# Hybrid decoder block: the first norm applied behind the first eight products instead of ahead of them

## The reference

```python
h  = rms_norm(x, norm_mix_w)             # x: 512 rows of 1024
proj = h @ w_in                          # gdn q k v z alpha beta, fox q k v f o, merge gates
qkv = silu(causal_depthwise_conv(concat(gq, gk, gv), conv_w))   # 4 taps, 24 tiles of 128 channels
...                                      # gated delta rule, forgetting attention, merge,
x = x + y @ w_out                        # second norm, SwiGLU, final norm
...
def rms_norm(x, w):                      # y = x * rsqrt(mean(x*x) + EPS) * w, by row
```

## Time and profile before

| | us |
|---|---|
| median of 3 runs (lowest to highest) | 1158.74 (1158.58 to 1159.56) |
| the profiled execution | 1158.56 |
| its span, first to last instruction | 1157.0 |
| TensorE busy | 1133.6 (98%) |
| VectorE, ScalarE, GpSimd busy | 526.9, 454.6, 551.1 |
| mean granted clock of TensorE | 0.999 of 2.4 GHz |

### The profile page before, as it was taken

One profiled execution on the slowest core, in us unless ns is written; L12 is line 12 of the kernel. 1 busy time (PEld: TensorE's weight loads), 2 busy tenths in 40 slices (PEclk: granted clock), 3 DMA queues, 4 the chain that ended last, 5 costly groups with the idle time before them and its releaser, 6 DMA issues.

```text
span 1157.0 us, 16593 instructions
## 1 busy us (share of the span) xinstructions
PE 1133.6 (98%) x5973; PEld 943.3 (82%) x5973; DVE 526.9 (46%) x1135; ACT 454.6 (39%) x744; POOL 551.1 (48%) x297
## 2 busy tenths in 40 slices
PE   6999999999999999999999999999999999999997
PEld 5778888888888888888888888887888888888886
DVE  4434446464738257777777662523333333330001
ACT  5354353434344365555555432234223323321112
POOL 5434456362626155556566554434444444434443
PEclk9999999999999999999999999999999999999999
DMA  6333333231313243323323273523333333322231
GB/s 195 85 85 99 91 100 98 68 92 55 101 56 92 73 123 87 99 83 94 95 86 95 73 236 109 149 88 87 96 91 102 97 91 99 101 91 91 92 109 73
DMA packets 169632, 113.61 MB, mean 98 GB/s; under 512 B 6257, under 2 KB 157922, under 8 KB 169586
## 3 DMA queue, kind: packets, MB, share of 16 engines
q1 hardware_dynamic: 163218, 98.26, 29.8%
q10 hardware_dynamic: 6368, 14.72, 3.5%
HBM read 104.54 MB, written 8.42 MB: 98 GB/s over the span
## 4 chain that ended last, share of the span: by engine, by line
PE 86%; DVE 5%; issue 4%; POOL 3%; ACT 1%; DMA 1%; SPq 0%; DVEq 0%; ACTq 0%; POOLq 0%
PE ps L1465 61%; PE ps L1879 10%; PE ps L1555 6%; PE ps L1447 4%; PE ps L1771 2%; POOL w_lo L558 1%; PE ps L1738 1%; DVE ps L1180 1%; PE ps L1739 1%; DVE prod L1190 1%; POOL probs L651 1%; PE ps L1815 1%; DVE Wb L1195 1%; PE ps L1509 1%; DMA prm_rows<-in_gdn_norm_w 1%
## 5 line engine op out<-in xcount | busy, mean ns | idle before, releaser
L558 POOL TENSOR_TENSOR w_lo<-raw,w_hi 128x1024 fp32r<-128x1024 f32 x170 | 416.4, 2449 | 521.7 <-ACT w_hi L685 521.7
L1465 PE MATMUL ps<-h_hi,w_hi 128*128 128x512 f32 x976 | 384.6, 394 | 1.0 <-POOL w_lo L558 1.0
L1465 PE MATMUL ps<-h_hi,w_lo 128*128 128x512 f32 x976 | 384.0, 393 | 0.0
L1465 PE MATMUL ps<-h_lo,w_hi 128*128 128x512 f32 x976 | 383.0, 392 | 0.0
L685 ACT ACTIVATE w_hi<-raw 128x1024 fp32r<-128x1024 f32 x170 | 180.2, 1060 | 468.1 <-PE ps L1465 368.6
L1465 PEld LDWEIGHTS ps<-h_hi,w_hi 128*128 128x128 f32 x976 | 183.5, 188 | 39.6 <-issue 1.9
L1465 PEld LDWEIGHTS ps<-h_hi,w_lo 128*128 128x128 f32 x976 | 183.4, 188 | 36.8 <-issue 0.2
L1465 PEld LDWEIGHTS ps<-h_lo,w_hi 128*128 128x128 f32 x976 | 183.5, 188 | 36.1
L1056 DVE SCALAR_TENSOR_TENSOR tmp<-ps,prm,tmp 128x511 f32<-128x511 f32 (+2 forms) x72 | 53.9, 748 | 80.5 <-ACT tmp L715 75.4
L651 POOL TENSOR_SCALAR probs<-probs,rsum 128x128 f32<-128x128 f32 (+1 forms) x64 | 70.3, 1117 | 13.4 <-DVE rsum L1285 12.6
L1025 DVE TENSOR_SCALAR ms<-ss 128x1 f32<-128x1 f32 x8 | 1.2, 154 | 126.5 <-ACT raw L998 117.4
(11 more groups left out here) (268 smaller groups left out, 1557.1 us busy)
## 6 DMA issues: line engine op xcount, KB each, us to landing
raw<-in_w_in SPq DMA_DIRECT2D x80, 512.0 KB, 3.9
raw<-in_w_gate SPq DMA_DIRECT2D x22, 512.0 KB, 3.8
raw<-in_w_up SPq DMA_DIRECT2D x22, 512.0 KB, 3.8
raw<-in_w_down SPq DMA_DIRECT2D x22, 512.0 KB, 3.3
gate_dram<-gate ACTq DMA_DIRECT2D x24, 256.0 KB, 2.0
cumb<-cum_dram ACTq DMA_DIRECT2D x8, 512.0 KB, 3.5
raw<-in_w_branch_a SPq DMA_DIRECT2D x8, 512.0 KB, 3.9
raw<-in_w_branch_b SPq DMA_DIRECT2D x8, 512.0 KB, 3.9
```

Source lines behind the costliest of these rows:

```text
L558: pool.tensor_tensor(w_lo[:, r % 2, :], raw[:, r, :], w_hi[:, r % 2, :], ALU.subtract)\
L1465: return pe.matmul(ps[:, bank, :], wts[wl][k], acts[xl][:, k, :], start=(n == 0), stop=(n == len(PASSES) - 1))
```

## The change

The turned x is no longer normed ahead of its use. The blocks of x are turned as they are, split into new halves `hr_hi` and `hr_lo` (norm weight included, row factor not), and the first eight units (convs 0 and 1 with r from 0 to 3) and the small unit work on those. Their results are scaled by the row factors on the way out: VectorE multiplies the PSUM bank in place by `row_rstd` (the same 512 numbers on all partitions), the small sums by `rstd`. TensorE makes the row inside unit 1, as in the second norm. The normed halves `h_hi` and `h_lo`, which all later units use, are built behind the first eight: GpSimd adds the raw halves into `hs`, three slots (`raw_sum`), VectorE scales a slot, ScalarE takes the high half, VectorE the low half; `NORMED` says in which conv each of the eight k-tiles is done. The parameter rows are loaded from ScalarE's queue. The first weight tile's high half is made by VectorE. On SP the loads of weight tiles 1 to 3 stand ahead of those of `wsm`. On GpSimd the constants come ahead of the power and of the low halves; on VectorE the splitting of `wsm` comes behind convs 0 and 1. TensorE waits for the last two low halves at unit 8. Later counts of the same semaphores are moved up to match, and some tensors change place.

```diff
@@ sync @@
+        NORMED = ((0,), (1, 2), (3,), (4,), (5,), (6,), (7,), ())
...
-            for row, src in ((0, conv_w[0].rearrange("w (n p) -> (w n) p", p=P)),
...
-                sp.dma_start(prm_rows[row:row + src.shape[0], :], src).then_inc(prm_loaded, 16)
...
+            for r in range(1, 4):
+                load(0, r, col_tile(w_in, r * P), True)
             sp.dma_start(wsm[:, :, 0:2 * H], w_cols[:, :, GA:GA + 2 * H]).then_inc(small_loaded, 16)
             sp.dma_start(wsm[:, :, 2 * H:32], w_cols[:, :, FF:FF + FH]).then_inc(small_loaded, 16)
-            for r in range(1, 4):
-                load(0, r, col_tile(w_in, r * P), True)
@@ gpsimd @@
-            row_power(0)
-            row_power(1)
...
-            row_power(2)
-            row_power(3)
-            low_part(QKV0, 0)
...
-            for r in range(1, 4):
-                low_part(QKV0, r)
-            units(QKV0 + 1, NCONV // 4 - 1)
+
+            def raw_sum(k):
+
+                if k >= 3:
+                    pool.wait_ge(h_low, KT + k - 2)
+                pool.wait_ge(h_low, k + 1)
+                pool.tensor_tensor(hs[:, k % 3, :], hr_hi[:, k, :].bitcast(F32), hr_lo[:, k, :].bitcast(F32), ALU.add)\
+                    .then_inc(hs_ready, 1)
+
+            low_part(QKV0, 0)
+            low_part(QKV0, 1)
+            pool.wait_ge(ms_ready, TT)
+            power(rstd[:, 0:TT], ms[:, 0:TT], TT).then_inc(rstd_ready, TT)
+            low_part(QKV0, 2)
+            raw_sum(0)
+            raw_sum(1)
+            for r in range(3, 8):
+                raw_sum(r - 1)
+                low_part(QKV0 + r // 4, r % 4)
+            raw_sum(7)
+            units(QKV0 + 2, NCONV // 4 - 2)
@@ scalar @@
+            for row, src in ((0, conv_w[0].rearrange("w (n p) -> (w n) p", p=P)),
...
+                act.dma_start(prm_rows[row:row + src.shape[0], :], src).then_inc(prm_loaded, 16)
             act.wait_ge(prm_turned, 1)
             act.activation(prm[:, 0:NPRM], ps[:, 7, 0:NPRM], ACT.Copy).then_inc(prm_ready, 1)
-            high_part(0, 0, True)
+            for t in range(TT - 1):
+                square(t)
             act.wait_ge(prm_ready, 1)
-            norm_high(NMIX)
+            for k in range(KT):
+                act.wait_ge(x_turned, k + 1)
+                act.activation(hr_hi[:, k, :], ps[:, k, :], ACT.Copy,
+                               scale=prm[:, NMIX + k:NMIX + k + 1]).then_inc(h_high, 1)
+            act.wait_ge(w_high, 1)
             high_part(0, 1, True)
...
+            square(TT - 1)
...
+            def conv(q, r, first=False, raw_h=False):
                 high_ahead(q, r)
-                act.wait_ge(unit_done, 4 * q + r + 1)
+                if raw_h:
+                    if first and r == 0:
+                        act.wait_ge(wide_done, 1)
+                        act.activation(row_rstd[:, :], ps[:, 7, :], ACT.Copy).then_inc(wide_ready, 1)
+                    act.wait_ge(conv_scaled, 4 * q + r + 1)
+                else:
+                    act.wait_ge(unit_done, 4 * q + r + 1)
...
                                scale=prm[:, bass.ds(4 * q + (3 * NCONV + r), 1)]).then_inc(conv_seed, 1)
+                for k in NORMED[4 * q + r] if raw_h else ():
+                    act.wait_ge(hs_scaled, k + 1)
+                    act.activation(h_hi[:, k, :], hs[:, k % 3, :], ACT.Copy).then_inc(h_high, 1)
@@ vector @@
-            for t in range(TT):
-                dve.wait_ge(sq_summed, t + 1)
-                mean_square(t, t)
-                if t > 0:
-                    scale_row(t - 1)
-            scale_row(TT - 1)
-            norm_low(0, NMIX)
...
+            dve.wait_ge(w_loaded[0], 16)
+            copy(w_hi[:, 0, :], raw[:, 0, :]).then_inc(w_high, 1)
+            for k in range(KT):
+                dve.wait_ge(h_high, k + 1)
+                dve.scalar_tensor_tensor(out=hr_lo[:, k, :], in0=ps[:, k, :], scalar=prm[:, NMIX + k:NMIX + k + 1],
+                                         in1=hr_hi[:, k, :].bitcast(F32), op0=ALU.mult, op1=ALU.subtract)\
+                    .then_inc(h_low, 1)
+            dve.wait_ge(sq_summed, TT)
+            dve.tensor_scalar(ms[:, 0:TT], ss[:, 0:TT], 1.0 / D, EPS, ALU.mult, ALU.add).then_inc(ms_ready, TT)
...
+            diagonal(diag_ready)
+
+            def conv(q, r, raw_h=False):
+                if raw_h:
+                    dve.wait_ge(wide_ready, 1)
+                    dve.wait_ge(unit_done, 4 * q + r + 1)
+                    dve.tensor_tensor(ps[:, r, :], ps[:, r, :], row_rstd[:, :], ALU.mult).then_inc(conv_scaled, 1)
+                    for k in NORMED[4 * q + r]:
+                        dve.wait_ge(hs_ready, k + 1)
+                        dve.tensor_tensor(hs[:, k % 3, :], hs[:, k % 3, :], row_rstd[:, :], ALU.mult)\
+                            .then_inc(hs_scaled, 1)
                 dve.wait_ge(conv_seed, q * 4 + r + 1)
...
+                for k in NORMED[4 * q + r] if raw_h else ():
+                    dve.wait_ge(h_high, KT + k + 1)
+                    dve.tensor_tensor(h_lo[:, k, :], hs[:, k % 3, :], h_hi[:, k, :].bitcast(F32), ALU.subtract)\
+                        .then_inc(h_low, 1)
+
+            conv(0, 0, True)
+            conv(0, 1, True)
+            dve.wait_ge(small_loaded, 16 * 5)
+            copy(wsm_both[:, :, 0:32], wsm[:, :, :]).then_inc(wsm_high, 1)
...
+            for r in range(2, 4):
+                conv(0, r, True)
...
+                    dve.tensor_tensor(sums, sums, rstd[:, 0:TT].unsqueeze(2).broadcast_to([P, TT, 32]), ALU.mult)\
+                        .then_inc(small_taken, 1)
@@ tensor @@
-                    pe.wait_ge(x_scaled, t + 1)
+                    pe.wait_ge(x_loaded[t], 16)
...
+            def row_factor():
+                pe.wait_ge(consts_ready, 12)
+                pe.wait_ge(diag_ready, 1)
+                pe.matmul(ps[:, 7, :], step[:, 4 * P:5 * P], tmp[:, 0, :], start=True, stop=True).then_inc(wide_done, 1)
...
+                    if r == 1 and at == 18:
+                        row_factor()
...
+            pe.wait_ge(h_low, 2 * KT - 1)
             for r in range(4):
-                conv(2, r)
+                conv(2, r, False, (h_low, 2 * KT) if r == 0 else None)
```

More of the change, by code:

```diff
@@ L167, in hybrid_block @@
             sums = Lc[:, :, :].rearrange("p h s -> p (h s)").rearrange("p (t n) -> p t n", t=TT)
-            smT = Kd[0:64, 0:4, :].rearrange("p a n -> p (a n)")
+            smT = gate[0:64, 0, :]
         with ExitStack() as part:
@@ L721, in _ @@
             for r in range(4):
-                conv(0, r, True)
+                conv(0, r, True, True)
             act.wait_ge(small_unit, 1)
@@ L1011, in split, with norm_low @@
                 dve.tensor_tensor(lo, src, hi.bitcast(F32), ALU.subtract).then_inc(low_, 1)
-            def norm_low(n, col, kept=False):
+            def norm_low(n, col):
                 for k in range(KT):
                     dve.wait_ge(h_high, KT * n + k + 1)
-                    dve.scalar_tensor_tensor(out=h_lo[:, k, :], in0=ps[:, k % (4 if kept else KT), :],
+                    dve.scalar_tensor_tensor(out=h_lo[:, k, :], in0=ps[:, k % 4, :],
                                              scalar=prm[:, col + k:col + k + 1],
@@ L1019, in norm_low @@
                                              op1=ALU.subtract).then_inc(h_low, 1)
[L1020 to L1021 removed]
+                    copy(x2T[:, k, :], ps[:, k % 4, :]).then_inc(x2_copied, 1)
             def mean_square(t, col):
@@ L1051, in conv @@
-            def conv(q, r):
+            dve.wait_ge(w_loaded[0], 16)
[6 more added lines that the diff above has]
+            dve.wait_ge(sq_summed, TT)
@@ L1455, in turn_rows @@
                             pe.wait_ge(prm_ready, 1)
-                        last = turn(ps[:, k, t * P:(t + 1) * P], xn[:, t, k * P:(k + 1) * P])
+                        last = turn(ps[:, k, t * P:(t + 1) * P], x_nat[:, t, k * P:(k + 1) * P])
                         if t == TT - 1:
@@ L1490, in _, with conv @@
             turn_rows()
-            def conv(q, r):
+            def conv(q, r, raw_h=False, last_h=None):
                 pe.wait_ge(conv_bank, q * 4 + r + 1)
-                unit(q, r, h_hi, h_lo)
+                unit(q, r, hr_hi if raw_h else h_hi, hr_lo if raw_h else h_lo, (), last_h)
+            def row_factor():
+                pe.wait_ge(consts_ready, 12)
+                pe.wait_ge(diag_ready, 1)
+                pe.matmul(ps[:, 7, :], step[:, 4 * P:5 * P], tmp[:, 0, :], start=True, stop=True).then_inc(wide_done, 1)
             def first_conv(r, lag):
@@ L1508, in first_conv @@
                     wl, xl, k = PASSES[n]
-                    last = pe.matmul(ps[:, r, :], slot(r)[wl][k], (h_hi, h_lo)[xl][:, k, :], start=(at == 0),
+                    last = pe.matmul(ps[:, r, :], slot(r)[wl][k], (hr_hi, hr_lo)[xl][:, k, :], start=(at == 0),
                                      stop=(at == len(order) - 1))
@@ L1515, in _ @@
             for r in range(2, 4):
```

(14 more changed lines are left out.)

87 lines of the change are left out of this document (39 added, 48 removed).

## The result

The changed kernel takes **1162.12 us** (median of 8 runs, 1161.2 to 1162.97), the kernel before 1158.66 in the same runs (8 runs, 1158.17 to 1160.01). The ratio is 1.0028, 95% interval 1.0020 to 1.0037: slower by some 3.4 us. Forecast were 1163.7 and a range of 1157.5 to 1166.3. Its own profiled execution took 1162.0, with a span of 1160.3, against 1158.56 and 1157.0.

The account below looks back on a forecast made before the run. TensorE, busy 98% of the span, was taken as the bound, with time winnable only where it waits. The 3.49 us head start was lost to blocked VectorE work: unit 8 +5.0, so 1158.74 + 5.0 = 1163.7, range 1157.5 to 1166.3.

Parts of the forecast that it names:

- The prologue: Before unit 0: without row scalings and the parameter wait, unit 0 starts at 13.15, unit 1 at 19.27, a 3.49 us gain.
- rival of a slow start: TensorE before and in unit 0: first 12 matmuls at half pace add 2.0 us, giving 1165.7; chance 12%.
- The new chain through conv 0: Norm row product at 23.35, copied by 25.12, bank scaled by 25.84, then hs 0; mean, power and diagonal work hidden.
- A scaling under GpSimd: VectorE instructions with two SBUF inputs wait for a running GpSimd instruction and end 0.5 us behind it.
- The sum, unit by unit: Through the first units: unit 3 at 34.0, small unit 41.4, unit 4 45.1, unit 5 51.4, unit 8 71.3, +5.0 us.
- Convs 4 and 5: From unit 5's start: hs 6 waits for GpSimd to 9.8, taps of conv 5 at 61.2, unit 8 at 71.3.
- The likeliest case: The full sum, with all expected blocks: unit 8 +5.0 us, time 1163.7, alone 1162.7 to 1164.7; chance 40%.
- some of it blocks: The small subtraction or hs 6 escapes GpSimd, not both: +2.3 to +3 us, 1161.4; chance 22%.
- Nothing blocks: VectorE's scalings run free of GpSimd: unit 3 at 33.2, net -0.4 us, 1158.3; chance 20%.
- it pays: The prologue's head start survives, conv 0's chain being 2 us shorter: -2.5 to -3.5 us, 1155.7; chance 6%.

Follow-up runs that it names:

- The added transposes: Twenty transposes of ident put before x's: in the changed kernel 1162.6 us; in the kernel with both repairs and a 171-line pad 1158.85 us.
- The row early: Changed kernel with seven instructions moved so that the norm row is made during unit 0 and copied before unit 2's high half: 1158.3 us, ratio 0.9996.
- hs out of PSUM: Changed kernel with VectorE's scaling of hs reading the norm row from PSUM bank 7 instead of SBUF: 1159.24 us, ratio 1.0005.
- both together: Changed kernel with the norm row made during unit 0 and the hs scalings reading it from PSUM: 1157.73 us, ratio 0.9989.
- the kernel with the parameter rows alone: Kernel before, with only the load of the parameter rows moved from SP's queue to ScalarE's: 1159.86 us, ratio 1.001.
- the tiles moved too: Norm row made early, hs scaled from PSUM, and the pad before hr_hi and hr_lo lengthened from 170 lines: 1157.23 us with 171, 1157.2 with 173.
- the kernel with 171 lines: Changed kernel with norm row made early, hs scaled from PSUM, and the pad before hr_hi and hr_lo 171 lines, not 170: 1157.23 us, ratio 0.9986.

## Why the prediction was right in sign, and where its steps failed

*The prologue.* Unit 0 was put at 13.15 and came at 13.16, but by two errors that cancel. The first tile landed at 10.22, not 11.48 (bounds 10.9 and 12.0): without the parameter rows on its queue SP issues the tile at 2.67, not at 4.21. And x was not turned by 10.1 but by 12.2: 18 transposes at 0.21, then 14 at 0.11. The added transposes showed that this pace is TensorE's state at the start, not x's arrival. The prediction saw the same pace in the earlier trace rows, and used it only for its rival of a slow start; it took the mean of 0.999 for a sign that TensorE is fast from the first microseconds, which the trace has no entry for (before: the first is at 13.74). The row there is not that of the last twelve transposes: in the kernel before the first 16 stand 0.21 apart, the last 16, from 13.77 on, 0.11. This is also the part that differs between executions: unit 0 starts anywhere from 12.97 to 14.06 in profiles of the same prologue.

*The new chain through conv 0.* Its size was 0.6 too small. The product came at 23.96, not 23.35. 0.17 of it is unit 1's start and the slower pace; the rest is the wait for the diagonal, since the fourth square ended at 18.25 and not near 17.3, and mean and diagonal ran under GpSimd (1.36 and 2.87), a wait that the prediction declared hidden "with 6 us to go". The row early is worth 3.8 us, so this chain was the largest single cause; hs out of PSUM is worth 2.9, both together 4.4, since a chain that starts early enough escapes most of what the blocks cost.

*A scaling under GpSimd.* Right, rule and price, up to conv 5. hs 0, hs 1 and 2 and the small subtraction took 1.66, 3.43 and 2.54; expected were waits to 27.2, 34.4 and 41.3, measured 28.0, 35.0 and 41.6. With hs out of PSUM the time falls by 2.9. The Trainium skill (SBUF — State Buffer, section "SBUF: two separate sides") holds here: it names VectorE instructions with two SBUF inputs, and the eight scalings with one of the two in PSUM took 0.67 to 0.68.

*The sum, unit by unit.* Unit 3 at 34.61 (34.0), small unit 41.71 (41.4), unit 4 at 45.41 (45.1), unit 5 at 51.68 (51.4): each 0.3 to 0.6 late. The terms under these sums were not all right: two that were missing, the slow matmuls of unit 3 and the pace, were covered up to there by the wait for the small weights.

*Convs 4 and 5: the step that failed.* "GpSimd took its next low half at 6.84, so hs 6 waits to 9.8." Measured from unit 5's start VectorE asks at 7.09 and GpSimd at 7.08. The small sums were done earlier than in my sum (bank scaling at 6.49, not 6.7). GpSimd came 0.24 later, since unit 5 took 5.68 us, not 5.44: 0.11 is its first matmul, which the row shows as 0.50 long, 0.13 the slower pace. On the tie VectorE went first, as in two other profiles (both at 55.15; both at 59.68), so here a distance of 0.01 us decided, which nobody foresaw. The taps start 7.94 behind unit 5 in place of 9.8, 1.86 less; with the 0.3 above that leaves 1.56 at unit 8, the 1.6 by which 1163.7 was too high. The likeliest case was the wrong one of two neighbours: the rival "some of it blocks" is what took place, at 1162.1 where it was put at 1161.4, most of the difference being the 0.3 to 0.6 of the chain through conv 0.

*Slow TensorE at the start*: it came, but not at unit 0, where it was priced. It came at the transposes and, by idle time, at unit 3 (and at unit 0 in the kernel with the parameter rows alone). *Nothing blocks* and *it pays* did not happen; with the blocks and the late row repaired the gain is 1.2, with the tiles moved too 1.5 to 1.9. That it isn't 3.5 has its reason mostly in unit 0. In the kernel with 171 lines unit 0 starts 3.15 earlier than before and unit 1 1.73 earlier (21.03), since unit 0 takes 7.54 us with the row built inside it. Another 0.28 goes ahead of unit 8: with the two added scalings conv 5's taps start 7.78 behind unit 5, not 7.50, the gates' work puts unit 8's high half 6.46 to 6.48 behind these taps in all 14 profiles, and TensorE idles 1.29 there, not 1.01. That leaves 1.46 at unit 8 (64.85 against 66.31).

## What to carry to other kernels

A chain that is moved earlier runs beside other work than before: go through each of its instructions, the small ones too, and ask what GpSimd does at that moment; an operand read from PSUM, or a place between two GpSimd instructions, is worth more than the instruction's own time. Before believing a term that is "hidden", and before dropping one whose removal brings nothing, take away the other cause that ends at the same place: the slow matmuls and the small weights here each looked free alone. And compare the distance between matmuls of a tile that is new with that of the old one; 0.005 us apiece is invisible in a row and 1 us in 200 of them.
